# Moving the conditioning sums of a three-layer block onto VectorE and into the weight ring, with ring slots handled in halves

## The reference

```python
for l in range(2):                                     # first block
    q, k, v, gu, gv = split(rms_norm(x, norm1_g[l]) @ w_in[l])
    attn = banded_window_attention(rope(q), rope(k), v, sink[l])
    sgu = chunked_spatial_gating(gelu(gu), gelu(gv), ...)
    x = x + concat(rms_norm(attn), rms_norm(sgu)) @ w_o[l]
    a = depthwise_conv_centred(rms_norm(x, norm2_g[l]) @ w_up[l], conv_w[l], conv_b[l])
    g, u = split(a)                                    # 5632 each
    x = x + (silu(g) * u) @ w_down[l]
# second block, one layer
mod   = silu(c)     @ w_ada + b_ada                    # 2048 -> 6 * 2048
mod_c = silu(c_ctx) @ w_ada + b_ada
sh1, sc1, g1, sh2, sc2, g2 = split(mod)
csh1, csc1, ...            = split(mod_c)              # only these two are used
hc = rmsnorm(ctx) * (1 + csc1) + csh1
hl = rmsnorm(x) * (1 + sc1) + sh1
x = x + g1 * token_mixer(hl, states of hc)
x = x + g2 * mlp(rmsnorm(x) * (1 + sc2) + sh2)
return rmsnorm(x, final_norm_w)
```

## Time and profile before

| | |
|---|---|
| three runs | 4002.96, 4009.72, 4010.01 us; median 4009.72 |
| span of the profiled execution | 4009.0 us, first to last instruction; no other time of it is recorded |
| TensorE, VectorE, ScalarE, GpSimd busy | 3717.9, 2477.5, 1747.8, 646.0 us |
| mean granted clock of TensorE | 0.948 of the full one |
| moved by DMA | 687.26 MB |

### The profile page before, as it was taken

One profiled execution on the slowest core, in us unless ns is written; L12 is line 12 of the kernel. 1 busy time (PEld: TensorE's weight loads), 2 busy tenths in 40 slices (PEclk: granted clock), 3 DMA queues, 4 the chain that ended last, 5 costly groups with the idle time before them and its releaser, 6 DMA issues.

```text
span 4009.0 us, 44645 instructions
## 1 busy us (share of the span) xinstructions
PE 3717.9 (93%) x16234; PEld 2965.1 (74%) x16234; DVE 2477.5 (62%) x2262; ACT 1747.8 (44%) x1927; POOL 646.0 (16%) x379
## 2 busy tenths in 40 slices
...
GB/s 193 168 109 172 226 228 245 221 229 184 178 187 158 168 115 163 228 239 224 226 224 205 164 186 137 82 105 179 194 0 0 134 139 180 187 180 186 180 186 147
DMA packets 349116, 687.26 MB, mean 171 GB/s; under 512 B 15935, under 2 KB 20048, under 8 KB 347728
## 3 DMA queue, kind: packets, MB, share of 16 engines
...
## 4 chain that ended last, share of the span: by engine, by line
issue 47%; PE 24%; DVE 11%; DVEq 7%; POOLq 5%; DMA 3%; ACT 2%; ACTq 1%; POOL 1%; SPq 0%
POOLq L588 5%; DVE ada_sum L1105 4%; DVEq L1318 4%; PE acc L1994 3%; PE acc L1995 3%; PE acc L1996 3%; PE acc L1778 3%; PE acc L1780 3%; PE acc L1779 3%; DMA ada_raw<-in_w_ada 2%; DVE w_lo L1048 2%; DVEq L1295 2%; PE acc L2231 1%; PE side L2241 1%; DVE conv L1294 1%
## 5 line engine op out<-in xcount | busy, mean ns | idle before, releaser
L1048 DVE TENSOR_TENSOR w_lo<-w_raw,w_hi 128x2048 fp32r<-128x2048 f32 x362 | 816.2, 2258 | 568.1 <-ACT w_hi L621 567.5
L621 ACT ACTIVATE w_hi<-w_raw 128x2048 fp32r<-128x2048 f32 x362 | 678.6, 1879 | 569.8 <-DMA w_raw<-in_w_down 273.6
L1778 PE MATMUL acc<-w_hi,in_h 128*128 128x512 f32 x2112 | 866.0, 410 | 15.2 <-DVE in_l L1057 12.9
L1779 PE MATMUL acc<-w_lo,in_h 128*128 128x512 f32 x2112 | 855.2, 405 | 0.0
L1780 PE MATMUL acc<-w_hi,in_l 128*128 128x512 f32 x2112 | 854.0, 404 | 0.0
L587 POOL TENSOR_TENSOR ada_sum<-ada_sum,ada_term 128x512 f32<-128x512 f32 x330 | 553.4, 1677 | 393.0 <-ACT ada_term L793 351.7
L1105 DVE SCALAR_TENSOR_TENSOR ada_sum<-ada_raw,silu_c,ada_sum 128x512 f32<-128x512 f32 x330 | 487.6, 1478 | 36.0 <-issue 11.0
L1778 PEld LDWEIGHTS acc<-w_hi,in_h 128*128 128x128 f32 x2112 | 410.6, 194 | 116.2 <-issue 14.4
L1780 PEld LDWEIGHTS acc<-w_hi,in_l 128*128 128x128 f32 x2112 | 409.3, 194 | 101.2
L1779 PEld LDWEIGHTS acc<-w_lo,in_h 128*128 128x128 f32 x2112 | 410.6, 194 | 97.3
L1741 DVE TENSOR_TENSOR w_lo<-w_raw,w_hi 128x2048 fp32r<-128x2048 f32 x126 | 288.4, 2291 | 293.2 <-ACT w_hi L1024 293.2
...
## 6 DMA issues: line engine op xcount, KB each, us to landing
w_raw<-in_w_up SPq DMA_DIRECT2D x176, 1024.0 KB, 5.1
w_raw<-in_w_mlp SPq DMA_DIRECT2D x128, 1024.0 KB, 5.3
w_raw<-in_w_in SPq DMA_DIRECT2D x100, 1024.0 KB, 5.1
ada_raw<-in_w_ada ACTq DMA_DIRECT2D x176, 512.0 KB, 4.4
w_raw<-in_w_down SPq DMA_DIRECT2D x64, 1024.0 KB, 5.1
w_raw<-in_w_o SPq DMA_DIRECT2D x32, 1024.0 KB, 5.1
...
w_raw<-in_w_out SPq DMA_DIRECT2D x16, 1024.0 KB, 5.1
```

Source lines behind the costliest of these rows:

```text
L621: nc.scalar.activation(hi[s][:, 0:n], raw[s][:, 0:n], ACT.Copy).then_inc(w_hi[s], 1)
L1048: nc.vector.tensor_tensor(lo[s][:, 0:n], raw[s][:, 0:n], hi[s][:, 0:n].bitcast(F32), ALU.subtract).then_inc(w_lo[s], 1)
L1778: nc.tensor.matmul(acc[p][i][:], ah_[:, kt, tok], hi[s][:, k], start=(kt == 0), stop=False)
L1779: nc.tensor.matmul(acc[p][i][:], ah_[:, kt, tok], lo[s][:, k], start=False, stop=False)
```

## The change

The sums for c and c_ctx are both taken by VectorE, from ring slots, as ordinary pieces of the ring that ScalarE and TensorE skip. 44 such pieces per layer stand among the others: six in in, four in out, two per pair in up, three per chunk of down. So a sum takes two pairs in the up stage. Only the first eight sums are taken for both vectors (`ADA_BOTH`), the other fourteen for c alone. The dedicated buffers, ScalarE's terms and transfers and GpSimd's additions are gone. Every semaphore of the ring is doubled, one for each half of a slot (two k-tiles): a half is loaded, rounded, subtracted, awaited and released by itself, in the last layer too. Down has eleven pieces of four. The layers, out and down are written out; the pairs 1 to 10 are a loop over two. Two small tiles move.

```diff
+    IN_ORDER = [
+        ["p0", "p1", "a0", "p2", "a1", "p3"], ["p0", "p1", "p2", "a2", "p3"], ["p0", "p1", "p2", "p3"], ["p0", "p1", "p2", "p3"],
+        ["p0", "p1", "p2", "a3", "p3"], ["p0", "p1", "p2", "a4", "p3"], ["p0", "p1", "p2", "a5", "p3"],
+    ]
+    O_ORDER = [["p0", "p1", f"a{6 + c}", "p2", "p3"] for c in range(4)]
+    UP_ORDER = ["p0", "p1", "p2", "a0", "p3", "p4", "p5", "p6", "a1", "p7"]
+    DN_ORDER = [
+        ["p0", "p1", f"a{32 + 3 * c}", "p2", "p3", "p4", f"a{33 + 3 * c}", "p5", "p6", "p7", f"a{34 + 3 * c}", "p8", "p9", "p10"] for c in range(4)
+    ]
+    ADA_LAYER, ADA_SINGLE, ADA_UP = 11, 10, 12
+    ADA_BOTH = 8
...
         def piece(src, s, r, n=4):
-            sp.wait_ge(w_free[s], r)
-            sp.dma_start(raw[s][:, 0:n], src).then_inc(w_loaded[s], 16)
+            for h in range(2):
+                ks = slice(2 * h, min(2 * h + 2, n))
+                sp.wait_ge(w_free[s][h], r)
+                sp.dma_start(raw[s][:, ks], src[:, ks]).then_inc(w_loaded[s][h], 16)
...
+        def ada_half(s, r, q, half, vectors):
+
+            for k in range(2 * half, 2 * half + 2):
+                dve.drain()
+                if k == 2 * half:
+                    dve.wait_ge(w_loaded[s][half], r * 16)
+                for v in range(vectors):
+                    c = silu_c[:, v, 4 * q + k:4 * q + k + 1]
+                    if 4 * q + k == 0:
+                        a = nc.vector.tensor_scalar(ada_sum[v][:], raw[s][:, k], c, None, ALU.mult)
+                    else:
+                        a = nc.vector.scalar_tensor_tensor(ada_sum[v][:], raw[s][:, k], c, ada_sum[v][:], ALU.mult, ALU.add)
+            a.then_inc(w_hi[s][half], 1)
+            dve.drain().then_inc(w_lo[s][half], 1)
+            dve.sem_inc(w_free[s][half], 1)
+            if (q, half) == (3, 1):
+                dve.sem_inc(ada_sums, 1)
...
+                if c in (1, 4, 5, 6):
+                    ada(l, {1: 2, 4: 3, 5: 4, 6: 5}[c], 0)
...
                 split_up(2)
                 if before is not None:
                     finish_pair(before)
+                ada_up(0, 0)
                 split_up(3)
-                ada_piece(0)
+                ada_up(0, 1)
                 split_up(4)
-                ada_piece(1)
                 split_up(5)
-                ada_piece(2)
                 split_up(6)
-                ada_piece(3)
                 outer_taps(j, 0)
+                ada_up(1, 0)
                 split_up(7)
-                ada_piece(4)
+                ada_up(1, 1)
                 split_up(8)
-                ada_piece(5)
                 split_up(9)
-                ada_piece(6)
-                ada_piece(7)
...
+                if k % 2 == 0:
+                    pe.wait_ge(w_lo[s][k // 2], r)
```

More of the change, by code:

```diff
@@ L294, in program @@
     assert UL % 2 == 0
-    ADA_PIECES = KT // 2
     AL = [8 + 4 + 2 * NPAIR + 2, 8 + 4 + 2 * NPAIR + 6]
-    DN_SIZES = [4] * 8 + [3] * 4
-    DN_AT = [sum(DN_SIZES[:i]) for i in range(12)]
+    DN = FT // 4
     IN_COLS = [0, 1024, 512, 2560, 3072, 1536, 2048]
@@ L448, in _ @@
         sp.dma_start(ctx_first[:], t["ctx_2"][0].rearrange("(t p) d -> p t d", p=P)).then_inc(x_loaded, 16)
-        with sp.Fori(0, 2) as l:
+        for l in range(2):
             for b in range(2):
@@ L460, in _, with ada_load @@
                 sp.dma_start(staged[0:88, 2 + k], src).then_inc(staged_in, 16)
+            def ada_load(a):
+                piece(rows(w_ada2, a % 4 * CH, 4, (l * ADA_LAYER + a // 4) * CH), *place(ADA_AT[l, a]))
             for c, col in enumerate(IN_COLS):
-                for s in range(NS):
-                    piece(rows(w_in2, l * D + s * CH, 4, col), s, rnd(l, R_IN + c))
+                for what in IN_ORDER[c]:
+                    n = int(what[1:])
+                    if what[0] == "p":
+                        piece(rows(w_in2, l * D + n * CH, 4, col), *product_place(l, "in", c, n))
+                    else:
+                        ada_load(n)
                 if c == 0:
@@ L663, in _ @@
                 square_sum(ctx_first[:, i, c * CH:(c + 1) * CH], c_parts[:, i, c:c + 1]).then_inc(x_sq, 1)
-        with act_.Fori(0, 2) as l:
+        for l in range(2):
             act_.wait_ge(t_full[0], unit(l, U_TAB)[1])
@@ L1356, in _ @@
[L1356 to L1363 removed]
+                split_lo(*later_place(l, "dn", 0, i, 2))
+                if i in (1, 2, 4, 5, 7, 8):
+                    ada(l, 32 + (i - 1) // 3, (i - 1) % 3)
@@ L1780, in product, with ada_total @@
                     last = nc.tensor.matmul(acc[p][i][:], al_[:, kt, tok], hi[s][:, k], start=False, stop=(kt == ktn - 1))
-            last.then_inc(w_free[s], 1)
-        def ada_total(i):
+                if k % 2 == 1 or k == n - 1:
+                    last.then_inc(w_free[s][k // 2], 1)
+        def ada_total(i, both):
             pe.wait_ge(ada_mod, i + 1)
-            pe.wait_ge(a_used, i * ADA_PIECES + (ADA_PIECES + 2))
-            pe.wait_ge(term_used, i * KT + (KT + 2))
+            pe.wait_ge(ada_sums, i + 1)
+            n = 2 if both else 1
             for f in range(4):
-                for c in range(2):
-                    last = nc.tensor.matmul(side[0][:, 2 * f + c:2 * f + c + 1], ada_sum[c][:, f * P:(f + 1) * P], one[:], start=True, stop=True)
+                for c in range(n):
+                    last = nc.tensor.matmul(side[0][:, n * f + c:n * f + c + 1], ada_sum[c][:, f * P:(f + 1) * P], one[:], start=True, stop=True)
             last.then_inc(ada_post, 1)
```

516 lines of the change are left out of this document (267 added, 249 removed).

## The result

The changed kernel takes 3845.96 us (median of four runs, 3845.01 to 3848.18) against 4009.28 us for the kernel before (median of four runs): ratio 0.9598, 95% interval 0.9585 to 0.9612. I had forecast 3866 in a range of 3838 to 3945. The total is right by luck in part: as will be seen, a cost that I had some 85 us too small is cancelled by gains that I had some 107 us too small, 64 of them from something that is not in the sum at all. The profiled span went from 4009.0 to 3843.7 us, 165.3 less.

The account below looks back on a forecast made before the run. The prediction took TensorE as the bound, with slack in the up stages from VectorE and GpSimd disturbing each other and late ScalarE. Terms -147 - 14 + 10 + 11 - 4 = -144 us gave 3866 us, range 3838 to 3945.

Parts of the forecast that it names:

- Up pairs: Up stage, both layers: without GpSimd's and ScalarE's conditioning work TensorE sets the pace of each pair; 147 us gained.
- end of the up stage: End of both up stages: without the terms, y, `ah` and `al` stand directly behind the last matmul; 14 us gained.
- Totals: Totals for in, out and down now fall in stages where TensorE has no slack; 10 us cost.
- chunk 5 of in: In stage, chunks 5, 6 and 0: conditioning work ahead of scores, `attended` and a split delays TensorE; 11 us cost.
- Out and down: Out and down stages: VectorE's added operations stay hidden, 11.2 us from slot release to use against 6.7 needed; cost 0.
- rival 2: Ring too short: conditioning slots released late hold SyncE's later loads; 374 us for 88 pieces, 4240 us; chance 0.07.
- Halves: Some 550 more TensorE waits taken as 0, 28 us for the range; last layer gains 4 us, up to 20.
- Transfers: Loads in halves keep up, with 219 GB/s needed in an up pair; cost 0.
- Rival 1: Up stage of layer 0: piece p3 comes 1 to 3 us late in each pair; 3910 to 3940 us; chance 0.22.
- Rivals 3 and 4: Halves starve the transfers, 4103 us, chance 0.03; VectorE's 1.6 us operation is not GpSimd's doing, 4007 us, chance 0.02.

## Why the prediction was right, and where it was not

*Up pairs, -147 us, and end of the up stage, -14.* Right in cause and size. With the operands as slow as before, the changed kernel's up stages are 525.1 and 519.1 us, 175 less than before against my 161. 133 of these came with GpSimd's additions cut short alone. The operation takes 0.751 us everywhere, the clock is 1.00, VectorE is busy 412 and 359 us (I had 430 and 370), and TensorE starts 3.9 us behind the last matmul of the stage (I had 4). GpSimd is busy 26, not under 20. But one sentence of the prediction falls: that ScalarE's order, with y behind the terms, was part of the cause. Moving y ahead of the last two terms gave nothing. One reading was off too, though no term rests on it: a clock of 0.91 over a pair of 54.3 us, between the levels 1 and 0.5, is some 10 us at the low one and not 5; the granted clock was 0.50 from 478.7 to 488.9 us.

*Totals, +10, and chunk 5 of in, +11.* The waits for the score banks came (7.4 us in four, the longest 3.7 where I had 1.6 and 2.4), and so did one of 5.0 in chunk 6 where I had 1.2. The totals were not measured by themselves.

*Out and down, 0.* This is the step that failed. I followed one release to its use, found 11.2 us against 6.7, and called the rest hidden. Together with the term before, in, out and down were to cost 21 us; at equal rate of the matmuls they cost 106 to 118.7. The margin leaves out that SyncE issues in order, so that a slot freed late holds back every load behind it (6.0 us at 938.2); that ScalarE and VectorE do other ready work (`ah`, `al`, x, scores) only behind the piece they wait for; and that in these stages, unlike in up, some of that work is what TensorE wants next. This is the mechanism of rival 2, which I had priced at 374 us for 88 pieces. The 44 pieces of the up stages cost nothing to be seen, the other 44, by an estimate that takes off my 10 us for the totals, (118.7 - 10) / 44 = 2.5 us each. I had been right to give the mechanism a price and wrong to tie it to one chance for all stages.

*Halves, 0 in all but the last layer, where -4.* The 550 waits on TensorE cost nothing to be seen. What the halves give was missed: 304 us between this kernel and the one without them. In the last layer it is 18 us, inside my bound of 20; in the rest I had given it no bound at all. The last layer became 52.8 us shorter: about 25 with the operands in the slow place, 27 from the place.

*Transfers, 0.* Right for the up stage: 225 and 227 GB/s with 512 KB transfers against 228 with weights in 1024 KB and conditioning in 512 KB, and TensorE hardly waits. The Trainium skill, "DMA: Bandwidth & Descriptors", section Bandwidth, advises batches of 1 MiB or more for three quarters of the peak rate. The trace agrees only so far that the same rate took a DMA share of 0.71 against 0.67. In out and down the transfers are worth 18 us over both layers.

*Not in the sum at all: the matmuls' rate, -64 us.* I took the small tiles that move for nothing, and wrote that eleven pieces for twelve change no matmul. By rows 3 alone this could not be seen; that every stationary operand moved with `in_h` could. The run without it has 3907.7 us, inside the range but 42 us above the forecast. So it was luck that the forecast was met to 20 us: in, out and down cost 85 us more than the 21 I had (106 with both in a slow place); the place gave 64, the last layer 21, the up stages 14 and the rest some 7 more than I had.

*Rival 1* did not occur in the up stage: there is no stall above 0.9 us inside the up stage of layer 0. *Rivals 3 and 4* are refuted by 225 GB/s without waits and by 0.751 us.
